# A three-layer transformer stack on one core: head sums as two bulk-format products, waits by eighths, reciprocals and decay tables placed elsewhere

## The chip, the core and the metric

One core of a Trainium2 chip. Five engines work side by side, each through its own list of instructions, and meet only at semaphores: TensorE (PE, matrix products into PSUM), VectorE (DVE), ScalarE (ACT), GpSimd (POOL) and SyncE (SP), which here issues the weight transfers. The metric is the device time of one execution in microseconds; the profile is of one execution of its own, whose time stands beside its span below.

## The reference

A sequence of 512 tokens with 1024 features passes through one block of one kind and two of another. Cut to what matters here:

```python
h = rms_norm(x); proj = h @ w_in                     # block 1
o_attn = dilated_attention(q, k, v)                  # 24 heads of 64; q and k are normed head by head
o_gla  = rms_norm(gated_linear_attention(...)) * silu(r)
x += (gate0 * (o_attn @ w_attn_branch) + gate1 * (o_gla @ w_gla_branch)) @ w_out
x += square(relu(rms_norm(x) @ w_ff_up)) @ w_ff_down
# block 2, layer 0: window attention (8 q heads, 2 kv heads) and neighbourhood attention (8 heads),
#          q and k of both normed head by head;  x += concat(oa, ob) @ w_out_e;  x += mlp(x)
# block 2, layer 1: retention, both directions, 8 heads, decays from per-head rates:
dmask = where(allowed, exp(lg * max(diff, 0)), 0); cross = exp(lg * (pos + 1)); zeta = exp(lg * (127 - pos))
x += (silu(g) * groupnorm(y_f + y_b)) @ w_out_o;  x += mlp(x)
```

Norming q and k head by head means that for each column of 64 values `x * rsqrt(mean(x*x) + eps)` is needed: a sum of squares over each group of 64 features. "Head sum" below is this sum.

## The kernel before

The activations lie transposed in SBUF: `x` is eight tiles of 128 features by 512 tokens. The program runs stage by stage: `l1` (block 1's attention, gated linear attention (GLA), gates and mix), `ff0`, `l2` (window and neighbourhood attention), `ff1`, `l3` (retention), `ff2`.

**Units.** All dense products are cut into units of 128 output columns. A unit has 8 (some 4) slices of 128 inputs, and each slice takes three products in fp32r, the format in which the bulk of the work runs: weight high half by activation high half, high by low, low by high. That makes 24 (or 12) products into one PSUM bank, banks 0 and 1 in turn (`products`, L1529). SP loads a unit's weights, ACT makes their high halves (`split_hi`, L637), DVE their low halves (`split_lo`, L956), both two units ahead. DVE takes a finished unit out of PSUM (`evacuate`, L987, L977, L1008; `post` then finishes it, L1103 for what is added to `x`).

**Order within a step.** `pipeline` makes a list of steps (unit, unit before, parts) for each stage. Each engine walks through it in `static`, and what it does in a step has a fixed order written out in the code. On PE the "parts" (attention, GLA or retention work) and `shared_bank` (a head sum or a transpose of the unit before) are put between the unit's products at positions that `mark` computes; with a shared part the first position (`lead`) is after 10 products. On ACT a step begins with `split_hi` and then finishes the unit before; on DVE it begins with `evacuate`, then `split_lo`, then `post` and the parts.

**Head units.** 37 units are of kind "head": 24 in `l1` (dilated q and k), 5 "a" and 8 "b" in `l2`. DVE evacuates, ACT squares into `tmp` (L647), PE multiplies with `bones`, a matrix of two 64x64 blocks of ones, in fp32 (L1558) into bank 6 (`XB`), ACT takes logarithm and exponential (L649, L651), DVE multiplies (`post`, L1086).

**Dilated attention.** For each item of `l1` the parts are 0 (scores; `softmax` with the sum on DVE, exponentials on ACT, L740), 2 (`normalise`: DVE's reciprocal L1231, which releases POOL's multiplication L552 of the probabilities), 3 (transposes L1650 and their copies) and 1 (product with v, L1679; `head_lo` on DVE, L1238). In `static` of DVE the reciprocal of part 2 stands behind `split_lo`.

**Waits for whole operands.** `operands_ready` in PE's `static` waits before the first product of `w_gla_branch` for all eight output tiles of the GLA (`gl_out`, L1392), and before the three groups of `w_out_o_2` for 8, 12 and 16 tiles of the retention (`ret_out`, L1184). A unit of `w_gla_branch` is multiplied with its gate and added up on DVE, which ends in L1032.

**Layer 3.** `rates(0)` in the second step of `head(0)` has DVE make the exponents of all decay tables (`r_tab`; L1116 to L1131); ACT takes their exponentials in step 4. A retention head runs as six parts (`ret`), one to a step of a later unit; head 7's six go with the first six of the eight units of `w_out_o_2`'s second group.

Of the kernel before, what the change touches and what calls it, by code (L numbers as in the profile page):

```python
# [11 lines left out]
P = 128  # L12
# [51 lines left out]
def plan():  # L64
# [110 lines left out]
    todo = list(zip(head(0), [None, ("rates", 0), None, ("rates", 1), None, None]))  # L175
# [7 lines left out]
    todo += zip([("down", "w_out_o_2", D, P * j, 4, j) for j in range(KD)], ret[7] + [None] * 2)  # L183
# [9 lines left out]
def build(nc, a, out, units, steps):  # L193
    with ExitStack() as ctx:
# [19 lines left out]
        bones = sb("bones", [P, P])  # L214
# [5 lines left out]
        squares = stage[:, 0, :]  # L220
        psum = ctx.enter_context(nc.psum_tensor("psum", [P, 8, 512], F32))
# [16 lines left out]
        head_sq, up_hi, gate_abs = sem("head_sq"), sem("up_hi"), sem("gate_abs")  # L238
        gate_ln, gate_log, gate_exp = sem("gate_ln"), sem("gate_log"), sem("gate_exp")
# [224 lines left out]

        block = ctx.enter_context(nc.Block())
# [40 lines left out]
        def _(pool):  # L506
# [10 lines left out]
            done(pool.memset(bones[:, :], 0.0))  # L517
            for i in range(2):
                done(pool.memset(bones[64 * i:64 * i + 64, 64 * i:64 * i + 64], 1.0))
# [107 lines left out]
        def _(act):  # L627
# [11 lines left out]
            def continue_with(u, more=0):  # L639
# [3 lines left out]
                if u in EVACU and kind != "turn":  # L643
# [59 lines left out]
            def rates(i):  # L703
# [8 lines left out]
                else:  # L712
# [129 lines left out]
            def static(name):  # L842
# [108 lines left out]
        def _(dve):  # L951
# [36 lines left out]

            def post(u, f=0):
# [120 lines left out]
            def rates(i):  # L1110

                if i == 1:
                    return
                dve.wait_ge(rate_ready, 1)
                dve.wait_ge(dist_ready, 3)
                dve.scalar_tensor_tensor(out=r_lg, in0=r_lg, scalar=0.0, in1=r_lt, op0=ALU.min,  # L1116
                                         op1=ALU.subtract).then_inc(dve_step, 1)
                dve.wait_ge(dve_step, chain.up())
                dve.tensor_scalar(r_lt, r_lg, -1.0, None, ALU.mult).then_inc(dve_step, 1)
                dve.wait_ge(dve_step, chain.up())  # L1120

                for h in range(HEADS):
                    dve.tensor_scalar(r_tab[:, h, :], r_dist, r_lt[:, 8 + h:9 + h], None, ALU.mult)
                    dve.tensor_scalar(r_tab[:, HEADS + h, :], r_pos, r_lg[:, h:h + 1], None, ALU.mult)
                    dve.tensor_scalar(r_tab[:, 2 * HEADS + h, :], r_rev, r_lg[:, 8 + h:9 + h], None, ALU.mult)
                dve.tensor_scalar(r_z[:, 0:8], r_lg[:, 0:8], r_dist[:, P - 1:P], None, ALU.mult)
                dve.tensor_scalar(r_z[:, 8:16], r_lt[:, 8:16], r_dist[:, 0:1], None, ALU.mult)
                dve.tensor_scalar(r_z[:, 16:32], r_lg, float(P), None, ALU.mult).then_inc(dve_step, 1)
                dve.wait_ge(dve_step, chain.up())
                for h in range(HEADS):  # L1130
                    ins = dve.scalar_tensor_tensor(out=r_tab[:, h, :], in0=r_dist, scalar=r_lg[:, h:h + 1], in1=r_tab[:, h, :],  # L1131
                                                   op0=ALU.mult, op1=ALU.min)
# [780 lines left out]
```

## Time and profile before

| | us |
|---|---|
| median of 3 runs | 2435.39 (2432.76 to 2435.58) |
| the profiled execution | 2433.26 |
| its span, first to last instruction | 2431.5 |
| mean granted TensorE clock | 0.998 |
| busy: PE, DVE, ACT, POOL | 2388.0, 1261.3, 932.0, 135.4 |

How it is read: the page gives each engine's busy time, the chain of work that ended last, and the costliest groups of instructions by line. The trace behind it can be asked for the instructions of a stretch in order of time (start, duration, engine, line, output <- inputs, and in brackets how long the engine had stood before it and what released it), for what an engine waited for in sum, and for the busy time and granted clock in chosen windows. Matmuls are pipelined: a product's record is longer than the distance to the next one's start, and it is the distance that costs time.

### The profile page before, as it was taken

To read this page: it belongs to the slowest core of one execution; us is meant where nothing else is said; L and a number is where in the kernel's file an instruction comes from. 1 tells how busy PE (TensorE), PEld (TensorE's weight loads), DVE (VectorE), ACT (ScalarE), POOL (GpSimd) and SP (SyncE) were. 2 spreads that over 40 slices of the span, in tenths; PEclk is the share of its full clock that TensorE was granted. 3 is DMA by queue.
4 is the path that set the end of the run, shared out by engine and by line. 5 is a ranking of instruction groups with operands and counts; after the bars stand their busy time and mean duration, and the time that the engine had idled before them with its cause. 6 is when DMAs were issued, how large, how long until landed. Compare 5 with 4: busy or idle time off the path is not lost.

```text
span 2431.5 us, 32682 instructions
## 1 busy us (share of the span) xinstructions
PE 2388.0 (98%) x13012; PEld 1924.1 (79%) x13012; DVE 1261.3 (52%) x1853; ACT 932.0 (38%) x1459; POOL 135.4 (6%) x197
## 2 busy tenths in 40 slices
PE   8999999999999999998999999999999999999999
PEld 5777777787788888875678888887887887888887
DVE  5444444877653433546665344355655556534433
ACT  5343463446342332436654223343332223422321
POOL 3000000000000000042221000000000000100000
PEclk9999999999999999999999999999999999999999
DMA  4222213221323322331023233222222212333322
GB/s 148 71 69 70 70 51 98 77 72 62 104 87 98 107 89 95 104 96 44 23 83 111 89 95 104 88 94 78 70 78 78 87 53 67 110 100 105 95 86 78
DMA packets 60638, 205.79 MB, mean 85 GB/s; under 512 B 7249, under 2 KB 7249, under 8 KB 60386
## 3 DMA queue, kind: packets, MB, share of 16 engines
q1 hardware_dynamic: 59760, 202.93, 26.2%
q8 instruction: 86, 1.41, 0.2%
q10 hardware_dynamic: 754, 1.14, 0.2%
q14 instruction: 38, 0.31, 0.0%
HBM read 201.94 MB, written 2.10 MB: 84 GB/s over the span
## 4 chain that ended last, share of the span: by engine, by line
PE 90%; DVE 5%; ACT 4%; issue 1%; POOL 0%; DMA 0%; SPq 0%; POOLq 0%; DVEq 0%; ACTq 0%
PE psum L1529 79%; PE psum L1558 1%; PE psum L1583 1%; ACT arena L740 1%; PE psum L1554 1%; PE psum L1679 1%; PE psum L1590 1%; PE psum L1673 1%; PE psum L1650 1%; PE psum L1632 1%; DVE arena L1212 0%; DVE cols L1218 0%; ACT whi L637 0%; PE psum L1600 0%; PE psum L1596 0%
## 5 line engine op out<-in xcount | busy, mean ns | idle before, releaser
L1529 PE MATMUL psum<-hhi,whi 128*128 128x512 f32 x1640 | 648.5, 395 | 15.5 <-DVE wlo L956 9.0
L1529 PE MATMUL psum<-hlo,whi 128*128 128x512 f32 x1640 | 655.4, 400 | 0.0
L1529 PE MATMUL psum<-hhi,wlo 128*128 128x512 f32 x1640 | 644.4, 393 | 0.0
L1529 PE MATMUL psum<-uhi,whi 128*128 128x512 f32 x1392 | 548.9, 394 | 5.8 <-DVE arena L1008 2.9
L1529 PE MATMUL psum<-ulo,whi 128*128 128x512 f32 x1392 | 551.7, 396 | 0.0
L1529 PE MATMUL psum<-uhi,wlo 128*128 128x512 f32 x1392 | 547.5, 393 | 0.0
L956 DVE TENSOR_TENSOR wlo<-raw,whi 128x1024 fp32r<-128x1024 f32 (+1 forms) x399 | 465.5, 1167 | 63.3 <-ACT whi L921 31.6
L1529 PEld LDWEIGHTS psum<-hhi,whi 128*128 128x128 f32 x1640 | 308.7, 188 | 84.4 <-issue 14.4
L1529 PEld LDWEIGHTS psum<-hhi,wlo 128*128 128x128 f32 x1640 | 308.8, 188 | 70.1 <-issue 6.8
L1529 PEld LDWEIGHTS psum<-hlo,whi 128*128 128x128 f32 x1640 | 309.1, 188 | 67.9 <-issue 6.7
L921 ACT CAST whi<-raw 128x1024 fp32r<-128x1024 f32 x190 | 199.7, 1051 | 351.9 <-PE psum L1529 351.9
L1529 PEld LDWEIGHTS psum<-uhi,whi 128*128 128x128 f32 x1392 | 262.2, 188 | 66.4 <-issue 8.9
L1529 PEld LDWEIGHTS psum<-uhi,wlo 128*128 128x128 f32 x1392 | 262.2, 188 | 57.6 <-issue 4.9
L1529 PEld LDWEIGHTS psum<-ulo,whi 128*128 128x128 f32 x1392 | 262.2, 188 | 57.2 <-issue 5.1
L1103 DVE TENSOR_TENSOR x<-x,psum 128x512 f32<-128x512 f32 x144 | 99.0, 687 | 352.8 <-PE psum L1529 352.5
L637 ACT CAST whi<-raw 128x1024 fp32r<-128x1024 f32 (+1 forms) x209 | 200.0, 963 | 212.6 <-PE psum L1529 212.5
L977 DVE SCALAR_TENSOR_TENSOR stage<-psum,rstd 128x512 f32<-128x512 f32 x96 | 66.4, 692 | 265.9 <-PE psum L1529 255.5
L665 ACT ACTIVATE tmp<-stage 128x512 f32<-128x512 f32 x96 | 60.7, 632 | 310.5 <-DVE stage L977 310.5
L987 DVE TENSOR_TENSOR stage<-psum,rstd 128x512 f32<-128x512 f32 (+1 forms) x118 | 85.5, 724 | 130.5 <-PE psum L1529 126.9
L552 POOL TENSOR_TENSOR arena<-arena,cols 128x512 f32<-128x512 f32 (+4 forms) x48 | 58.6, 1220 | 384.1 <-DVE cols L1231 383.9
L1107 DVE TENSOR_TENSOR hlo<-tmp,hhi 128x512 fp32r<-128x512 f32 x96 | 66.5, 692 | 20.3 <-ACT hhi L667 20.3
L740 ACT ACTIVATE arena<-arena,cols 128x256 f32<-128x256 f32 (+4 forms) x96 | 52.1, 544 | 58.2 <-DVE cols L1216 58.2
(220 smaller groups left out, 1692.3 us busy)
## 6 DMA issues: line engine op xcount, KB each, us to landing
raw<-in_packed_dram SPq DMA_DIRECT2D x359, 512.0 KB, 3.6
raw<-in_packed_dram SPq DMA_DIRECT2D x40, 256.0 KB, 2.5
x<-in_xt_dram SPq DMA_DIRECT2D x8, 256.0 KB, 8.1
out_dram<-x SPq DMA_DIRECT2D x8, 256.0 KB, 2.0
arena<-in_near_bias_dram ACTq DMA_DIRECT2D x1, 1024.0 KB, 5.7
vec<-in_vec_dram ACTq DMA_DIRECT2D x1, 44.0 KB, 4.1
arena<-in_gla_gate_up_dram ACTq DMA_DIRECT2D x1, 32.0 KB
arena<-in_gla_gate_bias_dram ACTq DMA_DIRECT2D x1, 2.0 KB
```

The lines of the kernel that those rows point to most:

```text
L552: pool.tensor_tensor(p, p, part, ALU.mult).then_inc(att_norm, 1)
L637: nc.scalar.copy(whi[:, u % 4, 0:kt, :], raw[:, u % 4, 0:kt, :]).then_inc(hi_done, 1)
L665: nc.scalar.activation(t, s, ACT.Square).then_inc(act_step, 1)
L740: ins = nc.scalar.activation(p[:, i, :], p[:, i, :], ACT.Exp, bias=c[:, i:i + 1], accum_out=c[:, 2 + i:3 + i])
L921: nc.scalar.copy(whi[:, u % 4, :, :], raw[:, u % 4, :, :]).then_inc(hi_done, 1)
L956: dve.tensor_tensor(wlo[:, u % 4, 0:kt, :], raw[:, u % 4, 0:kt, :], whi[:, u % 4, 0:kt, :].bitcast(F32), ALU.subtract).then_inc(lo_done, 1)
L977: dve.scalar_tensor_tensor(out=s, in0=g, scalar=0.0, in1=rstd, op0=ALU.max, op1=ALU.mult).then_inc(evacuated, 1)
L987: dve.tensor_tensor(s, g, r, ALU.mult).then_inc(evacuated, 1)
L1103: dve.tensor_tensor(x[:, j, :], x[:, j, :], g, ALU.add).then_inc(posted, 1)
L1107: dve.tensor_tensor(lo[:, j, :], tmp[:, u % 2, :], hi[:, j, :].bitcast(F32), ALU.subtract)\
L1529: mm = pe.matmul(g, w[:, u % 4, k, :], v[:, k, :], start=n == 0, stop=n == 3 * kt - 1)
L1554: mm = pe.transpose(XB[:, P * t:P * t + P], src, ident[:, :])
```

## The change

It does six things.

1. **Head sum in two products of fp32r.** ACT squares the evacuated unit into a high half (the last tile of the operand buffer that is free in that stage), DVE multiplies the unit with itself in fp32 into `tmp` and subtracts the high half, which gives the low half. PE multiplies `bones` (now fp32r, copied once by DVE) with the high, then the low half, into the same bank.
2. **Order on ACT and DVE.** ACT's square comes ahead of `split_hi`; DVE's multiplication and subtraction come ahead of `split_lo`.
3. **Lead.** With a head unit before, the shared part stands after 13 products instead of 10.
4. **Reciprocals.** In `l1` the reciprocal of part 2 comes ahead of these squares instead of behind `split_lo`.
5. **Waits by eighths.** The full waits of `operands_ready` go; each slice of the first unit waits for its own tile.
6. **Retention.** `rates` is spread over four steps (1 to 4 of `head(0)`), ACT's exponentials remain in the last of them; head 7's parts go with units 0, 2, 4 (two of them), 5 and 6.

```diff
-    todo = list(zip(head(0), [None, ("rates", 0), None, ("rates", 1), None, None]))
+    todo = list(zip(head(0), [None] + [("rates", i) for i in range(4)] + [None]))
...
-    todo += zip([("down", "w_out_o_2", D, P * j, 4, j) for j in range(KD)], ret[7] + [None] * 2)
+    r = ret[7]
+    todo += zip([("down", "w_out_o_2", D, P * j, 4, j) for j in range(KD)],
+                [r[0], None, r[1], None, [r[2], r[3]], r[4], r[5], None])
...
+        def head_squares(u):
+            hi, lo = first_operand if units[u][5][0] in ("a", "b") else second_operand
+            return hi[:, KD - 1, :], lo[:, KD - 1, :]
...
-                    nc.scalar.activation(t, s, ACT.Square).then_inc(head_sq, 1)
...
+            def square_head(u):                                  # ACT
+                act.wait_ge(evacuated, EVACU[u] + 1)
+                nc.scalar.activation(head_squares(u)[0], stage[:, u % 2, :], ACT.Square).then_inc(head_sq, 1)
...
                 for u, prev, parts in steps[name]:               # ACT static
+                    if prev is not None and units[prev][0] == "head":
+                        square_head(prev)
                     if u is not None:
                         split_hi(u + 2)
...
+            def square_head(u):                                  # DVE
+                s, t = stage[:, u % 2, :], tmp[:, u % 2, :]
+                hi, lo = head_squares(u)
+                dve.wait_ge(evacuated, EVACU[u] + 1)
+                dve.tensor_tensor(t, s, s, ALU.mult).then_inc(dve_step, 1)
+                dve.wait_ge(dve_step, chain.up())
+                dve.wait_ge(head_sq, HEADU[u] + 1)
+                dve.tensor_tensor(lo, t, hi.bitcast(F32), ALU.subtract).then_inc(head_low, 1)
...
                     if prev is not None:                         # DVE static
                         evacuate(prev)
+                    for part in parts:
+                        if part[:2] == ("att", "dil") and part[3] == 2:
+                            normalise(run_at["dil"] + part[2])
+                    if prev is not None and units[prev][0] == "head":
+                        square_head(prev)
...
                         split_lo(u + 2, kt=units[u + 2][4])
-                    for part in parts:
-                        if part[:2] == ("att", "dil") and part[3] == 2:
-                            normalise(run_at["dil"] + part[2])
...
+                    if u in outputs_before and part == 0:        # PE products
+                        pe.wait_ge(ret_out, outputs_before[u] + k + 1)
+                    if u == gla_branch0 and part == 0:
+                        pe.wait_ge(gl_out, k + 1)
...
-                    pe.matmul(XB, bones[:, :], tmp[:, u % 2, :], start=True, stop=True).then_inc(head_sum, 1)
+                    pe.matmul(XB, bones[:, :], hi, start=True, stop=False)
+                    pe.wait_ge(head_low, HEADU[u] + 1)
+                    pe.matmul(XB, bones[:, :], lo, start=False, stop=True).then_inc(head_sum, 1)
...
-                    lead = 10 if shared and not soon else 0
+                    lead = 0 if soon or not shared else 13 if units[prev][0] == "head" else 10
```

In `rates`, step 0 now makes the rates and the small columns (5 operations), step 1 the 16 operations of `cross` and `zeta`, step 2 eight of the mask's exponents, step 3 the eight L1131.

## Rows read from the trace of the kernel before

**Rows 1.** The page: busy time by engine, and the chain by engine.
```profile
PE 2388.0 (98%) x13012; PEld 1924.1 (79%) x13012; DVE 1261.3 (52%) x1853; ACT 932.0 (38%) x1459; POOL 135.4 (6%) x197
...
PE 90%; DVE 5%; ACT 4%; issue 1%; POOL 0%; DMA 0%; SPq 0%; POOLq 0%; DVEq 0%; ACTq 0%
```
**Rows 2.** PE's waits: line, releaser: us in total, times, longest.
```profile
PE psum L1558 <- ACT tmp L647: 8.0, 6, 3.2
...
PE psum L1759 <- DVE arena L1341: 2.4, 1, 2.4
...
PE psum L1650 <- POOL arena L552: 1.5, 3, 0.6
```
**Rows 3.** Timeline of PE, layer 1: start, us, engine, line, out<-in.
```profile
78.78 0.39 PE L1529 MATMUL psum<-hhi,whi 128*128 128x512 f32 x1
...
79.69 1.02 PE L1558 MATMUL psum<-tmp,bones 128*128 128x512 f32 x2
...
80.78 0.40 PE L1529 MATMUL psum<-hhi,wlo 128*128 128x512 f32 x1
```
**Rows 4.** Groups by line and form: count, busy, mean ns, idle before.
```profile
L1107 DVE TENSOR_TENSOR hlo<-tmp,hhi 128x512 fp32r<-128x512 f32 x96 | 66.5, 692 | 20.3 <-ACT hhi L667 20.3
...
L647 ACT ACTIVATE tmp<-stage 128x512 f32<-128x512 f32 x37 | 23.3, 630 | 24.5 <-DVE stage L987 24.2
```
**Rows 5.** Timeline of PE, DVE and POOL in a step with a reciprocal.
```profile
101.07 0.39 PE L1529 MATMUL psum<-hhi,whi 128*128 128x512 f32 x1
...
101.64 0.68 DVE L987 TENSOR_TENSOR stage<-psum,rstd 128x512 f32<-128x512 f32 x1
...
103.61 1.47 POOL L552 TENSOR_TENSOR arena<-arena,cols 128x768 f32<-128x768 f32 x1 [14.99 <-DVE cols L1231]
```
**Rows 6.** Timeline of DVE and POOL in layer 2 and behind it.
```profile
1089.67 0.71 DVE L1192 TENSOR_SCALAR arena<-arena 128x384 f32<-128x384 f32 x2
...
1112.21 1.45 DVE L1192 TENSOR_SCALAR arena<-arena 128x384 f32<-128x384 f32 x2
...
1112.38 1.08 POOL L552 TENSOR_TENSOR arena<-arena,cols 128x512 f32<-128x512 f32 x1 [4.06 <-DVE cols L1231]
...
1278.52 1.44 POOL L613 TENSOR_TENSOR stage<-stage,tmp 128x512 f32<-128x512 f32 x1 [1.41 <-ACT tmp L886]
...
1279.51 1.00 DVE L1442 SCALAR_TENSOR_TENSOR ulo<-x,vec,uhi 128x512 fp32r<-128x512 f32 x1
```
**Rows 7.** Layer 3: timeline of DVE and PE, then a window's busy times, PEclk, DMA.
```profile
1642.28 0.29 DVE L1123 TENSOR_SCALAR arena<-arena 128x128 f32<-128x128 f32 x1
...
1649.56 1.22 DVE L956 TENSOR_TENSOR wlo<-raw,whi 128x1024 fp32r<-128x1024 f32 x1
...
1648.23 0.39 PE L1529 MATMUL psum<-uhi,wlo 128*128 128x512 f32 x1
1651.53 0.77 PE L1529 MATMUL psum<-uhi,whi 128*128 128x512 f32 x1 [2.91 <-DVE arena L1008]
...
1651.00:1658.00 7.00, 6.47 (x18) 5.20 (x19) 3.05 (x5) 2.69 (x4) 0.00 (x0) 0.52 0.48 150
```
**Rows 8.** Timeline of PE at the first group of w_out_o_2.
```profile
1843.45 0.39 PE L1529 MATMUL psum<-uhi,wlo 128*128 128x512 f32 x1
1846.93 0.47 PE L1529 MATMUL psum<-hhi,whi 128*128 128x512 f32 x1 [3.09 <-DVE hlo L1184]
```
**Rows 9.** Timeline of PE and DVE at the last retention head.
```profile
2028.21 2.61 PE L1583 MATMUL psum<-arena 128*128 128x256 f32 x11 [2.59 <-issue]
...
2029.22 0.68 DVE L1103 TENSOR_TENSOR x<-x,psum 128x512 f32<-128x512 f32 x1
```
**Rows 10.** Timeline of PE, third unit of w_gla_branch.
```profile
621.84 0.47 PE L1529 MATMUL psum<-uhi,whi 128*128 128x512 f32 x1 [1.63 <-DVE hlo L1032]
```
**Rows 11.** Windows behind two other stalls: busy by engine, PEclk, DMA.
```profile
582.00:586.00 4.00, 3.09 (x10) 2.64 (x11) 3.61 (x6) 3.65 (x7) 0.00 (x0) 0.57 0.22 75
2020.00:2030.00 10.00, 7.20 (x37) 5.70 (x36) 8.47 (x16) 5.52 (x10) 0.00 (x0) 1.00 0.09 30
```

More of the change, by code:

```diff
@@ L213, in build @@
         ones = sb("ones", [P, P])
-        bones = sb("bones", [P, P])
+        bones = sb("bones", [P, P], F32R)
         vec = sb("vec", [P, VALL])
@@ L220, in build @@
         squares = stage[:, 0, :]
+        bones_in = arena[:, 16800:16800 + P]
         psum = ctx.enter_context(nc.psum_tensor("psum", [P, 8, 512], F32))
@@ L516, in _ @@
             done(pool.memset(const[:, 1:2], GN_EPS))
-            done(pool.memset(bones[:, :], 0.0))
+            done(pool.memset(bones_in, 0.0))
             for i in range(2):
-                done(pool.memset(bones[64 * i:64 * i + 64, 64 * i:64 * i + 64], 1.0))
+                done(pool.memset(bones_in[64 * i:64 * i + 64, 64 * i:64 * i + 64], 1.0))
             done(pool.memset(ident[:, :], 0.0))
@@ L642, in continue_with @@
                 s, t = stage[:, u % 2, :], tmp[:, u % 2, :]
-                if u in EVACU and kind != "turn":
+                if u in EVACU and kind not in ("turn", "head"):
                     act.wait_ge(evacuated, EVACU[u] + 1 + more)
                 if kind == "head":
-                    nc.scalar.activation(t, s, ACT.Square).then_inc(head_sq, 1)
                     act.wait_ge(head_sum, HEADU[u] + 1)
@@ L711, in rates @@
                     nc.scalar.activation(r_lt, r_lt, ACT.Ln, bias=1.0).then_inc(rate_ready, 1)
-                else:
+                if i == 3:
                     act.wait_ge(ret_exp, 1)
@@ L1110, in rates @@
             def rates(i):
-                if i == 1:
[L1113 to L1132, printed above, removed]
-                ins.then_inc(ret_exp, 1)
+                if i == 0:
+                    dve.wait_ge(rate_ready, 1)
+                    dve.wait_ge(dist_ready, 3)
+                    dve.scalar_tensor_tensor(out=r_lg, in0=r_lg, scalar=0.0, in1=r_lt, op0=ALU.min,
+                                             op1=ALU.subtract).then_inc(dve_step, 1)
+                    dve.wait_ge(dve_step, chain.up())
+                    dve.tensor_scalar(r_lt, r_lg, -1.0, None, ALU.mult).then_inc(dve_step, 1)
+                    dve.wait_ge(dve_step, chain.up())
+                    dve.tensor_scalar(r_z[:, 0:8], r_lg[:, 0:8], r_dist[:, P - 1:P], None, ALU.mult)
+                    dve.tensor_scalar(r_z[:, 8:16], r_lt[:, 8:16], r_dist[:, 0:1], None, ALU.mult)
+                    dve.tensor_scalar(r_z[:, 16:32], r_lg, float(P), None, ALU.mult)
@@ new lines, in rates @@
+                if i == 1:
+                    for h in range(HEADS):
+                        dve.tensor_scalar(r_tab[:, HEADS + h, :], r_pos, r_lg[:, h:h + 1], None, ALU.mult)
+                        dve.tensor_scalar(r_tab[:, 2 * HEADS + h, :], r_rev, r_lg[:, 8 + h:9 + h], None, ALU.mult)
+                if i == 2:
+                    for h in range(HEADS):
+                        ins = dve.tensor_scalar(r_tab[:, h, :], r_dist, r_lt[:, 8 + h:9 + h], None, ALU.mult)
+                    ins.then_inc(dve_step, 1)
+                    dve.wait_ge(dve_step, chain.up())
@@ L1135, in ret @@
+                if i == 3:
+                    for h in range(HEADS):
+                        ins = dve.scalar_tensor_tensor(out=r_tab[:, h, :], in0=r_dist, scalar=r_lg[:, h:h + 1],
+                                                       in1=r_tab[:, h, :], op0=ALU.mult, op1=ALU.min)
+                    ins.then_inc(ret_exp, 1)
             def ret(h, part):
@@ L1489, in _ @@
             dve.tensor_scalar(nbias[:, :], vec[:, b0:b0 + 16], -1.0, None, ALU.mult).then_inc(vec_ready, 1)
+            dve.tensor_copy(bones[:, :], bones_in).then_inc(bones_ready, 1)
             q_norms = vec[:, VROWS:VROWS + 6].rearrange("p (a b) -> p a b", b=2)[:, :, 0]
@@ L1510, in _ @@
                             UNIT_OF["down", "w_out_e_2", 512, 0]: "near"}
+            outputs_before = {UNIT_OF["down", "w_out_o_2", 0, 0]: 0, UNIT_OF["down", "w_out_o_2", D, 0]: 8,
+                              UNIT_OF["down", "w_out_o_2", D + 4 * P, 0]: 12}
             norm_before = {first(n[0]): i for i, n in enumerate(NORMS)}
@@ L1796, in _ @@
                      "shared_bank": shared_bank}
-            def operands_ready(u):
-                names = units[u][:4]
-                if names == ("branch", "w_gla_branch", 0, 0):
-                    pe.wait_ge(gl_out, 8)
-                if names == ("down", "w_out_o_2", 0, 0):
-                    pe.wait_ge(ret_out, 8)
-                if names == ("down", "w_out_o_2", D, 0):
-                    pe.wait_ge(ret_out, 12)
-                if names == ("down", "w_out_o_2", D + 4 * P, 0):
-                    pe.wait_ge(ret_out, 16)
             def mark(i, n, total, lead):
```

5 lines of the change are left out of this document (4 added, 1 removed).

## The prediction

> **What bounds the kernel now.** I read the page's busy shares and its chain of waits first: TensorE (PE) is busy 98% of the span and makes 90% of the chain, VectorE (DVE) 52%, ScalarE (ACT) 38%, GpSimd (POOL) 6% [rows 1]. So the time is PE's work plus the places where PE stands. Second, PE's waits, longest first: outside the start, which the change doesn't touch, PE stands in pieces of at most 3.2 us at a few dozen places [rows 2, 7 to 10]. Third, PE's timeline around one head sum, for what PE itself pays: products start 0.227 us apart (four from 78.78 to 79.69), and from the start of the head sum at 79.69 to the second product behind it 1.09 us go by; less one product that is 0.86 us for a head sum, two fp32 records [rows 3]. There are 37 of them. An edit brings something only if it makes PE's own work shorter or ends a stall that nothing else holds. The sum below is made against the profiled execution, 2433.26 us with a span of 2431.5. The median of the runs, 2435.39, lies 2.1 above it, which I add at the end.
>
> **Head sums, PE's side.** The fp32 pass (0.86) goes, two fp32r products come. The fp32r products here start 0.227 apart, so two cost 0.45; saved 0.41 each, 37 times: **15.2** gain. The trace has no fp32r product with this stationary matrix; the bounds are a price as now (0 saved) and 0.45, and I take 0.45, since form and sizes are those of the 128x512 products beside it.
>
> **Head sums, the other engines.** ACT's square (630 ns) is done ahead of the weight split instead of behind it. DVE gets a multiplication and a subtraction of 128x512 in front of its weight split; the like of it, two SBUF sources, takes 692 ns [rows 4]. PE now reaches the head sum 13 products into the unit and its second half at 14, that is 3.17 us after the unit begins. Evacuation of the unit before ends 1.25 us in at most where the attention isn't late [rows 5] (normally sooner), so the low half is there at 1.25 + 1.4 = 2.65: hidden by 0.5 us. The weight split that is queued behind them comes 1.4 later, but is for a unit two further on. Were all this cover gone, 37 x 1.4 = 52 us would appear; DVE's 52% speaks against it. The first heads of each stage, where the norm is late, gain a little: **0.5** (0 to 1).
>
> **Reciprocals ahead of the squares.** In nine of the 24 dilated heads (three in each of three groups) the item's reciprocal now stands directly in front of the multiplication and the subtraction. It releases POOL's normalising multiplication (L552), which in [rows 5] started in DVE's idle time and took 1.47 us. What the two engines do to each other is in [rows 6]: the pair of operations L1192 takes 0.71 us at 1089.67, with no L552 beside it, and 1.45 at 1112.21, where POOL's L552 (from 1112.38, 1.08 us) begins between the two; the second is through 0.2 behind POOL's end. And an L1442 under POOL's L613 takes 1.00, where the like takes 0.69 [rows 4], and ends 0.55 behind POOL's end, as if it had stood until then. I take this: the operation that comes second stands until the first is done. Then, for the middle head of three, counted from the unit's begin at 101.07: scores run 0.27 later than now (three products later, 0.68, less 0.41), so evacuation ends at 1.25 + 0.27 = 1.52, the reciprocal is through at 1.7, the multiplication (issued before POOL) at 2.4, POOL at 3.9, the subtraction at 4.6. PE wants it at 3.17: it stands 1.45. With the last head's longer L552 (1.68) and 0.15 later evacuation it is 1.8; with the first's shorter one (0.83) and its evacuation that is not held up by the attention, 0.35. Three of each, less what stands there now (0.2, 0, 0): **-0.5 - 4.35 - 5.4 = -10.2**. Bounds: 0 (no conflict) and -12.
>
> The Trainium skill ("SBUF — State Buffer", section "Who interferes with whom") says that a DVE instruction with two SBUF inputs and a GpSimd instruction that reads SBUF contend for a shared port pair, and that the one issued first keeps the other out. It speaks against this part of the change, and the rows agree with it: 10.2 us lost. If the added operations had one SBUF input each, by that rule nothing would be lost here.
>
> **Layer 2's eight 'b' heads.** PE stands 8.0 us in six pieces at the head sum, waiting for ACT's square, up to 3.2 [rows 2]. The square in front of the 1.05 us split takes about 0.8 to 1.0 off the larger ones; but DVE's two added operations delay the weight split, softmax and the masks that POOL makes there, which share the port. I take +4.3 and give back 3.3: **+1.0**, bounds -4 and +3.
>
> **GLA gates, first block.** Three stalls of PE behind POOL's L552, 1.5 us together [rows 2]: with the reciprocal ahead of the weight split the first goes, the others stay a little because POOL now meets the split's port use: **+1.0** (0 to 1.8).
>
> **Eighths.** For w_gla_branch PE may start as soon as the first eighth is out. But two units on it waits 1.63 us for L1032, a chain of ACT and DVE that does not hang on PE [rows 10]; starting earlier makes that wait longer by as much: **0** (0 to 0.8). For w_out_o_2, PE stands from 1843.45 + 0.23 to 1846.93, 3.25 us, for the last of eight outputs [rows 8]; this one is needed only with the last of the unit's eighths, 21 products = 4.8 us later. No other wait is listed at this place: **+3.25** (0 to 3.25).
>
> **Decay tables.** In the second step of layer 3 DVE works from 1642.28 to 1649.56 on tables (24 operations like the one of 1642.28, then 11 more), and the weight split and L1008 queue behind it; PE stands from 1648.23 + 0.23 to 1651.53, 3.07 us. After that the granted clock is 0.52, the lower of its two levels (1.2 GHz), in 1651 to 1658 [rows 7]: of the 6.47 us that PE is busy there, 0.48 each is lost, some 3.0 more (an estimate from this row). Spread over four steps, no step gets more than 16 of the 35 operations, 3.4 us of the 7.3, so L1008 is some 4 to 5 us sooner, ahead of 1648.2. The tables are first wanted by the first retention head, four units on; by the operations of each step they are ready shortly before PE comes there (0.4 us, an estimate from the spacing of the steps). Gain **6.0** (if the clock falls anyway or the tables are late: 3).
>
> **Last retention head.** PE's stall of 2.59 (L1583) is put down to issue; what it follows is the retention work on DVE [rows 9]. With the parts moved a step on, unit 2 begins not before L1103, which now ends at 2029.90, has freed the bank. PE had six products of the unit done and stood from about 2025.5; it would come to unit 2 at 2026.8 and stand to about 2030, 3.2 instead of 2.75: **-0.4** (-1.5 to 1.5). The copy of the bones at the start lies in DVE's idle time before the first norm: 0.
>
> **Sum**: 15.2 + 0.5 - 10.2 + 1.0 + 1.0 + 0 + 3.25 + 6.0 - 0.4 = 16.3. 2433.26 - 16.3 = 2417.0, and 2.1 to the median: **2419**.
>
> **The rivals.**
> *No conflict at the port.* The subtraction runs beside POOL, the nine stalls don't come: 10.2 better, **2408.8**. For it: no row shows a subtraction of this very form beside L552, and the order of arrival may differ. Against: both conflicts in [rows 6].
> *DVE binds in the attention parts.* The 1.4 us more per head on DVE delay softmax, scores and masks in layers 1 and 2 as well, each time by what the lower bounds above hold (-4 instead of +1 in layer 2, and 1 us more): **2425**.
> *The stalls of layer 3 move instead of going.* As with w_gla_branch, the next wait takes up the 9.25 us: **2428**.
> *No cheaper pass.* If two fp32r passes with the bones cost what one of fp32 costs, 15.2 goes and the rest (1.1) remains: **2434**, no change that can be told.
> *Slower: the clock falls behind the new stalls.* After the 3.07 stall in layer 3 and after the 2.4 us wait at L1341 the clock fell to its lower level for some us (0.52 and 0.57 [rows 2, 7, 11]), 3.0 lost at the first. If each of the nine new stalls of layer 1 did this, 26 us would be added: **2445**; it decides from the sixth such fall on (16.3 / 3.0). Against it: the stall of 2.59 in 2020 to 2030 left the clock at 1.00 [rows 11], and so would most of 0.35 to 1.8.
>
> **How the numbers follow.** Chances: the forecast (2413 to 2423) 0.50; no conflict 0.20; DVE binds 0.13; layer 3 gives back 0.08; no cheaper pass 0.04; slower 0.05. The range 2407 to 2428 takes in the first three cases, and half of the fourth, with the bounds of the layer 2 and layer 3 terms on either side. About 0.2% (4.9 us) is what a measurement of this kernel can tell from no change. Faster by more: the first four cases, less a little, 0.88; within: "no cheaper pass" and the edges of its neighbours, 0.07; slower: 0.05.
>
> **What would show it.** In the profile after: head sums with two products 0.23 apart instead of 0.86 in all (right), or still 0.4 apart (wrong). In layer 1, PE waits at the head sum's second product for DVE's subtraction, nine times, 1 to 2 us each, with an L552 in front of it on POOL: if these are missing, the conflict was misjudged and the time is near 2409. In layer 3 the waits on L1008 and L1184 gone, the granted clock at 1.00 in 1651 to 1658 and no new wait of their size within the next two units; if one is there, the gain moved. In layer 2 the head sum's waits for ACT under 4 us in sum. In the first block's branch the wait on L1032 longer by what the one before it lost. The prediction is wrong as a whole if the weight splits (L956) appear among PE's waits for more than a few us: then DVE's added work isn't covered.

## The result

| | before | after |
|---|---|---|
| median of 4 runs each, us | 2434.89 | 2419.93 (2419.79 to 2420.46) |
| ratio to before (95% interval) | | 0.994 (0.9923 to 0.9958) |
| profiled execution, us | 2433.26 | 2420.46 |
| its span, us | 2431.5 | 2418.5 |

The change makes the kernel 15.0 us faster by the medians and 12.8 by the two profiled executions; 2419 was forecast. One of the four executions of experiment 8 below took 4598.90 us at a granted clock of 0.911 and is left out of its median. The page's busy line and its chain, after:

```profile
PE 2374.2 (98%) x13012; PEld 1924.0 (80%) x13012; DVE 1322.5 (55%) x1928; ACT 932.9 (39%) x1459; POOL 152.6 (6%) x197
...
PE 86%; DVE 6%; ACT 4%; POOL 2%; issue 2%; DMA 0%; POOLq 0%; SPq 0%; DVEq 0%; ACTq 0%
```

Beside [rows 1]: PE works 13.8 us less, DVE 61 us more, and POOL 17 us more although it has the same 197 instructions. PE's share of the chain falls from 90% to 86%, POOL's rises from 0 to 2%. Most of this 2% is masks in layer 2 (L601, 32 us of the chain) and not the normalising that the forecast was about (L561, 4.9 us in layer 1, 4.4 before), so it is no sign of the nine stalls. Those show in PE's waits, after (in sum, times, longest):

```profile
...
PE psum L1602 <- DVE ulo L1010: 9.4, 10, 1.6
PE psum L1568 <- DVE x L1126: 4.4, 2, 3.1
PE psum L1568 <- DVE hlo L1055: 2.5, 1, 2.5
PE psum L1803 <- DVE arena L1368: 2.5, 1, 2.5
...
PE psum L1600 <- ACT hhi L679: 2.1, 2, 1.7
PE psum L1694 <- POOL arena L561: 1.9, 3, 1.3
```

Line numbers have moved: L1568 is the products' line (L1529 before), L1600 and L1602 the two products of the head sum, L1007 and L1010 DVE's multiplication and subtraction, L561 POOL's normalising (L552), L1126 the addition to `x` (L1103), L1055 the end of a branch unit (L1032). The head sum's wait for ACT fell from 8.0 [rows 2] to 2.1. The waits on L1008 and L1184 [rows 7, 8] are gone. New, and the largest but for the start, is the wait that was forecast: L1602 for the subtraction, nine of its ten times at the heads behind a reciprocal (9.2 of the 9.4 us). The weight splits (L970), whose appearance was to show the prediction wrong as a whole, hold PE up for 0.8 us beyond the 8.9 at the start (9.0 before): DVE's added work is covered there. Where the decay tables made PE stand in [rows 7], it now works through, at the full clock (after):

```profile
1643.00:1647.00 4.00, 4.00 (x22) 3.28 (x21) 3.08 (x5) 0.95 (x1) 0.00 (x0) 1.00 0.30 73
```

A head sum where nothing is late (timeline of PE, after): the two products are 0.22 and 0.23 apart from their neighbours, 0.45 for the sum, where [rows 3] had 0.86.

```profile
29.45 0.39 PE L1568 MATMUL psum<-hhi,whi 128*128 128x512 f32 x1
29.68 0.39 PE L1600 MATMUL psum<-uhi,bones 128*128 128x512 f32 x1
29.90 0.39 PE L1602 MATMUL psum<-ulo,bones 128*128 128x512 f32 x1
30.13 0.39 PE L1568 MATMUL psum<-hlo,whi 128*128 128x512 f32 x1
```

And a step with a reciprocal (all engines, after), to be read against [rows 5]:

```profile
97.90 0.69 DVE L1001 TENSOR_TENSOR stage<-psum,rstd 128x512 f32<-128x512 f32 x1
...
98.50 0.16 DVE L1258 RECIPROCAL cols<-cols 128x2 f32<-128x2 f32 x1
...
98.62 0.69 DVE L1007 TENSOR_TENSOR tmp<-stage 128x512 f32<-128x512 f32 x1
...
98.73 1.90 POOL L561 TENSOR_TENSOR arena<-arena,cols 128x768 f32<-128x768 f32 x1 [14.96 <-DVE cols L1258]
...
99.35 1.83 DVE L1010 TENSOR_TENSOR ulo<-tmp,uhi 128x512 fp32r<-128x512 f32 x1
...
99.62 0.39 PE L1600 MATMUL psum<-uhi,bones 128*128 128x512 f32 x1
...
101.24 0.50 PE L1602 MATMUL psum<-ulo,bones 128*128 128x512 f32 x1 [1.23 <-DVE ulo L1010]
```

The reciprocal releases POOL at 98.66, while the multiplication already runs. POOL's L561 takes 1.90 instead of 1.47, and the subtraction, issued at 99.35, takes 1.83 instead of 0.69 and ends 0.55 behind POOL's end at 100.63. PE stands 1.23 between the two products of one head sum. By the starts of the products this stall costs 1.50: 1.39 between the two, where 1.62 lie instead of 0.227, and 0.11 behind them, where 0.34 lie. A wait as the profile lists it begins at the end of a record of 0.39, and so leaves 0.27 of the stall's price out.

### The profile page after: what moved, and what is told of

Its sections match the earlier page's. It is cut to its first block, busy times and chain, and to the rows that moved or that the text cites. A ratio compares the mean times of both kernels' runs of the same rounds, so it can differ in the third digit from the quotient of the medians.

```text
span 2418.5 us, 32796 instructions
## 1 busy us (share of the span) xinstructions
PE 2374.2 (98%) x13012; PEld 1924.0 (80%) x13012; DVE 1322.5 (55%) x1928; ACT 932.9 (39%) x1459; POOL 152.6 (6%) x197
## 4 chain that ended last, share of the span: by engine, by line
PE 86%; DVE 6%; ACT 4%; POOL 2%; issue 2%; DMA 0%; POOLq 0%; SPq 0%; DVEq 0%; ACTq 0%
PE psum L1568 77%; POOL arena L601 1%; ACT arena L752 1%; PE psum L1627 1%; PE psum L1593 1%; DVE ulo L1010 1%; PE psum L1723 1%; PE psum L1694 1%; PE psum L1634 1%; DVE stage L1001 1%; PE psum L1676 1%; PE psum L1644 0%; PE psum L1640 0%; PE psum L1602 0%; DVE cols L1243 0%
## 5 line engine op out<-in xcount | busy, mean ns | idle before, releaser
L1568 PE MATMUL psum<-hhi,whi 128*128 128x512 f32 x1640 | 647.8, 395 | 15.4 <-DVE wlo L970 9.7
L1568 PE MATMUL psum<-hlo,whi 128*128 128x512 f32 x1640 | 645.0, 393 | 0.0
L1568 PE MATMUL psum<-hhi,wlo 128*128 128x512 f32 x1640 | 644.5, 393 | 0.0
L1568 PE MATMUL psum<-uhi,whi 128*128 128x512 f32 x1392 | 548.3, 394 | 3.1 <-DVE hlo L1055 2.5
L1568 PE MATMUL psum<-uhi,wlo 128*128 128x512 f32 x1392 | 545.7, 392 | 0.0
L1568 PE MATMUL psum<-ulo,whi 128*128 128x512 f32 x1392 | 545.0, 392 | 0.0
L970 DVE TENSOR_TENSOR wlo<-raw,whi 128x1024 fp32r<-128x1024 f32 (+1 forms) x399 | 465.8, 1168 | 60.7 <-ACT whi L935 31.5
L1568 PEld LDWEIGHTS psum<-hhi,whi 128*128 128x128 f32 x1640 | 308.6, 188 | 83.5 <-issue 10.9
L1568 PEld LDWEIGHTS psum<-hhi,wlo 128*128 128x128 f32 x1640 | 308.8, 188 | 64.7 <-issue 1.0
L1568 PEld LDWEIGHTS psum<-hlo,whi 128*128 128x128 f32 x1640 | 309.1, 189 | 63.6 <-issue 1.0
L1568 PEld LDWEIGHTS psum<-uhi,whi 128*128 128x128 f32 x1392 | 261.6, 188 | 62.7 <-issue 8.8
L1568 PEld LDWEIGHTS psum<-uhi,wlo 128*128 128x128 f32 x1392 | 261.6, 188 | 55.3 <-issue 1.8
L1568 PEld LDWEIGHTS psum<-ulo,whi 128*128 128x128 f32 x1392 | 261.8, 188 | 54.1 <-issue 2.0
L1126 DVE TENSOR_TENSOR x<-x,psum 128x512 f32<-128x512 f32 x144 | 98.9, 687 | 348.1 <-PE psum L1568 347.8
L561 POOL TENSOR_TENSOR arena<-arena,cols 128x512 f32<-128x512 f32 (+4 forms) x48 | 67.2, 1400 | 361.3 <-DVE cols L1258 361.1
```

Source lines behind the costliest of these rows:

```text
L561: pool.tensor_tensor(p, p, part, ALU.mult).then_inc(att_norm, 1)
L970: dve.tensor_tensor(wlo[:, u % 4, 0:kt, :], raw[:, u % 4, 0:kt, :], whi[:, u % 4, 0:kt, :].bitcast(F32), ALU.subtract).then_inc(lo_done, 1)
L1126: dve.tensor_tensor(x[:, j, :], x[:, j, :], g, ALU.add).then_inc(posted, 1)
L1568: mm = pe.matmul(g, w[:, u % 4, k, :], v[:, k, :], start=n == 0, stop=n == 3 * kt - 1)
```

## Where the time went, product by product

The dense products are the same in number and order in both kernels, so the distance between the same two products before and after gives what each part did (two profiled executions; positive is gained):

| part | forecast | measured |
|---|---|---|
| 37 head sums on PE | 15.2 | 16.6 (0.45 each) |
| first head of each stage | 0.5 | 0.3 |
| nine heads behind a reciprocal | -10.2 | -11.5 |
| layer 2, the eight 'b' heads beyond that | +1.0 | -1.3 |
| GLA gates | +1.0 | +1.35 |
| w_gla_branch by eighths | 0 | +0.86 - 0.90 = 0 |
| decay tables | 6.0 | 6.0 (3.07 of stall + 2.94 of clock) |
| first group of w_out_o_2 by eighths | 3.25 | 3.4 |
| last retention head | -0.4 | -2.1 |
| start and rest | 0 | 0.3 |
| sum | 16.3 | 13.1 |

All but two terms are within 1.4 us of the forecast. The two that are not, layer 2 and the last retention head, are where the granted clock fell after the change and hadn't before (experiments 3 and 7). The profiled execution of before lay 1.6 us below its median, that of after 0.5 above: the medians lie 15.0 apart and the profiles 12.8, so 2419.9 and 2419 agree better than the sums behind them (16.3 and 13.1).

## The experiments

Each kernel is the changed one with one edit, unless said otherwise. Medians are of runs beside the kernel before on the same chip. Theory: the nine stalls are a conflict of DVE's subtraction with POOL's normalising; the other losses are the granted clock. Rivals: DVE's queue alone; stalls alone.

**1. The square in PSUM.**

```diff
-                s, t = stage[:, u % 2, :], tmp[:, u % 2, :]
+                s, t = stage[:, u % 2, :], psum[:, u % 2, :]
...
-                    if u - 2 in EVACU:
+                    if u - 2 in HEADU:
+                        pe.wait_ge(head_low, HEADU[u - 2] + 1)
+                    elif u - 2 in EVACU:
```

> The changed kernel, but DVE puts the product s*s into the PSUM bank of the unit just taken out instead of into SBUF, so that the subtraction has one SBUF source. Theory (the subtraction stands because POOL's L561 holds what both need for a second SBUF source): the subtraction takes 0.69 us beside L561 instead of 1.4 to 2.0, the nine waits at the head sum's second product in layer 1 (9.2 us, 11.2 by starts) shrink to 0.2 each, time about 2410. Rival (DVE's order is what makes them late, whatever the sources): the waits stay, 2420. In layer 2, where the masks run on POOL, the theory also lets some of the 2 us in waits there go.

2410.57 us (ratio 0.990, 0.9885 to 0.9915): 9.4 less than after. The same step:

```profile
97.90 0.15 DVE L1258 RECIPROCAL cols<-cols 128x2 f32<-128x2 f32 x1
...
98.01 0.70 DVE L1007 TENSOR_TENSOR psum<-stage 128x512 f32<-128x512 f32 x1
...
98.13 1.90 POOL L561 TENSOR_TENSOR arena<-arena,cols 128x768 f32<-128x768 f32 x1 [14.52 <-DVE cols L1258]
...
98.75 0.69 DVE L1010 TENSOR_TENSOR ulo<-psum,uhi 128x512 fp32r<-128x512 f32 x1
...
99.01 0.39 PE L1602 MATMUL psum<-uhi,bones 128*128 128x512 f32 x1
...
99.49 0.50 PE L1604 MATMUL psum<-ulo,bones 128*128 128x512 f32 x1
...
99.62 1.49 DVE L970 TENSOR_TENSOR wlo<-raw,whi 128x1024 fp32r<-128x1024 f32 x1 [0.18 <-ACT whi L646]
```

Order and number of instructions are the same; what has changed is where the product lies, which the multiplication writes and the subtraction reads (and PE waits for the subtraction before it fills that bank again; no wait of the profile is put down to this). The subtraction takes 0.69 in the middle of POOL's 1.90. Over all 24 heads its mean goes from 1.07 to 0.69 us, and PE's wait at the second product in 77 to 400 us from 9.2 to this:

```profile
PE psum L1604 <- DVE ulo L1010: 0.7, 3, 0.2
```

The rival is out: the conflict is between two SBUF sources on DVE and POOL. The weight split (two SBUF sources) still stands for 0.27 us at the end of POOL's instruction, 1.49 against 1.22, and L561 keeps its 1.90, since the multiplication still reads SBUF twice (experiment 11 takes it away). In layer 2, where the theory had hoped for some of 2 us, the profile gained 0.9, part of it because the clock was low for a shorter time there; the profile of experiment 12, with the clock as long down as after, gained 0.4.

**2. The reciprocal behind the weight split again.**

```diff
-                    for part in parts:
-                        if part[:2] == ("att", "dil") and part[3] == 2:
-                            normalise(run_at["dil"] + part[2])
                     if prev is not None and units[prev][0] == "head":
                         square_head(prev)
...
                         split_lo(u + 2, kt=units[u + 2][4])
+                    for part in parts:
+                        if part[:2] == ("att", "dil") and part[3] == 2:
+                            normalise(run_at["dil"] + part[2])
```

> The changed kernel with the reciprocals of the dilated attention behind the weight split again, as before the change. Theory: the nine waits at the head sum (11.2 by starts) go, but POOL now begins at about 4.6 us into the unit and PE stands at the transposes L1694 some 0.9 to 1.1 us in six steps: about 2415. Rival (POOL has nothing to do with it; the two added DVE operations alone are late): the nine waits stay and the transposes wait on top, 2425 or more.

2420.9 us: no gain. PE's waits in the first 290 us of layer 1 show that the place was right and the sum wrong:

```profile
PE psum L1694 <- POOL arena L561: 6.1, 6, 1.1
PE psum L1602 <- DVE ulo L1010: 1.0, 5, 0.2
```

The 9.2 at the head sum went down to 1.0, and 6.1 came at the transposes, each 0.9 to 1.1 as expected; the net is 2.1 by waits, and 0.8 by starts (there are more stalls, and each costs more than its wait), not the 5 that I had made of it by setting the losses by starts (11.2) against gains by waits. The GLA gates gave another 1.3 back. With the square in SBUF, POOL is either in the subtraction's way or late for the transposes; the reciprocal's place only chooses which.

**3. The last retention head as before.**

```diff
-                [r[0], None, r[1], None, [r[2], r[3]], r[4], r[5], None])
+                r + [None] * 2)
```

> The changed kernel with the last retention head's six parts on units 0 to 5 again. Theory (the lower clock level after the 3.1 us stall costs the 1.4 there, the stalls themselves 0.5): the granted clock stays at 1.00 in the 5 us behind the stall and the time is 1.9 lower, 2418. Rival (the clock falls behind any stall of this kind): 2419.5, with the clock at 0.66 behind the stall again.

2419.86 us in the median (2417.68 to 2420.96), which doesn't tell it from after; the profiled execution, 2417.68, is 2.8 below that of after, 2.1 of it in this place. What the clock did there (first line after, behind the stall that ends at 2014.87; second line this kernel, behind the one at 2012; busy by engine, PEclk, DMA):

```profile
2015.00:2020.00 5.00, 5.00 (x16) 4.04 (x17) 1.94 (x5) 0.00 (x0) 0.00 (x0) 0.66 0.36 105
```
```profile
2012.00:2017.00 5.00, 4.64 (x29) 4.36 (x30) 4.79 (x11) 0.48 (x1) 0.00 (x0) 1.00 0.18 52
```

So the 2.1 lost in the last retention head are some 0.5 of stall (3.07 instead of 2.59), as forecast, and some 1.6 of clock: seven products 0.43 apart behind it make 1.4. The profile of experiment 4 separates the two: PE stands 3.08 there, the clock stays at 1.00 in 2021 to 2026, and the place loses 0.4 against before. That this holds in every run isn't shown by a median that didn't move.

**4. Lead 10.** The head sum stands after 10 products of the next unit again: `lead = 0 if soon or not shared else 10`.

> The changed kernel with the head sum after 10 products of the next unit instead of 13. If the low half is ready 0.5 us early at 13, as I worked out (2.65 against 3.17 us), it is ready 0.15 late or just in time at 10: PE waits up to 0.2 us at each of the 15 undisturbed heads of layer 1 and more in layer 2; time 2420 to 2425. Rival (the attention behind the head sum gains 0.68 from the earlier scores): 2417 or less.

2424.83 us, 4.9 more than after, as expected (2420 to 2425). The three later products are worth that: with 10, PE waits longer at L1600 for ACT's square in layer 2 (2.9 us by starts there), and a little at each head of layer 1 (2 us there in all).

```profile
PE psum L1600 <- ACT hhi L679: 4.7, 4, 2.5
```

**5. Decay tables in one step.** The list of steps as before, all four parts of `rates` in part 0.

> The changed kernel with all of DVE's decay tables in one step again. Theory: 3.1 us of stall at L1031 or so come back and the granted clock falls to its lower level behind it, 6.0 together: 2426. Rival (the clock fell in the profile of before by chance and not behind this stall): only 3.1 come back, 2423, with the clock at 1.00 behind it.

2426.46 us, 6.5 more than after. Timeline of PE and the window behind:

```profile
1645.72 0.47 PE L1568 MATMUL psum<-uhi,whi 128*128 128x512 f32 x1 [2.91 <-DVE arena L1031]
```
```profile
1645.00:1650.00 5.00, 4.28 (x15) 3.46 (x15) 2.31 (x3) 2.89 (x4) 0.00 (x0) 0.68 0.62 175
```

The stall is the one of [rows 7] to the hundredth, and the clock falls behind it again, for a shorter time (3.1 and 1.7 by starts, 4.8 in the profile; 2.9 of clock before). Most of the other 1.2 by which the two profiles differ is a longer fall at the last retention head. The rival is out: the three profiles with this stall (before, 5, 9) have a fall behind it, the eleven without have none, and both parts of the 6.0 were real.

**6. Full waits.** In `products` the first product waits for all `kt` tiles of `gl_out` and `ret_out`.

> The changed kernel with the waits for whole operands again at w_gla_branch and w_out_o_2. Theory: w_out_o_2 costs its 3.25 again and w_gla_branch nothing, because the wait for L1055 two units on (2.5 us now) shrinks by what is lost ahead of it: 2423.2. Rival (w_gla_branch's eighths bring what they remove, 0.8): 2424.

2425.18 us, 5.2 more, and 2 above what was expected. At w_gla_branch the small stall comes back and the next one shrinks (PE, this kernel; after has none and 2.49):

```profile
607.84 0.47 PE L1568 MATMUL psum<-uhi,whi 128*128 128x512 f32 x1 [0.61 <-DVE ulo L1419]
...
620.59 0.47 PE L1568 MATMUL psum<-uhi,whi 128*128 128x512 f32 x1 [1.59 <-DVE hlo L1055]
```

0.61 + 1.59 against 2.49: the eighths of the GLA bring nothing, as forecast. At w_out_o_2 the 3.09 came back, and this time the clock fell behind it, 0.66, which it hadn't done in the profile of before; that cost 1.6 more by starts. The stall and the clock:

```profile
1834.47 0.47 PE L1568 MATMUL psum<-hhi,whi 128*128 128x512 f32 x1 [3.09 <-DVE hlo L1211]
```
```profile
1834.00:1839.00 5.00, 4.53 (x14) 3.64 (x14) 4.11 (x7) 1.89 (x3) 0.00 (x0) 0.66 0.24 87
```

**7. Fewer masks.** Four of the six calls of `within` on POOL taken out.

> The changed kernel with 32 of the 48 mask operations of POOL (L601) in layer 2 left out: the bias of the neighbourhood attention stays partly unmasked. Theory (layer 2 loses its gain because DVE's added operations and POOL's masks hold each other up, so that the first 'b' head's square and the first item's normalising are late, 1.7 and 1.35 us, and the granted clock falls to 0.5 to 0.7 behind these two): both waits shrink below 1 us in sum, the clock stays at 1.00 from 1090 to 1108, and layer 2 is 4 to 5 us shorter, time about 2415. Rival (the chain from exponentials to square to head sum is that long by itself): the waits stay and the time is within 1 us of 2420.

2418.64 us, 1.3 less. Between theory and rival: the wait of 1.35 at the transposes went, the one at the first 'b' head's square stayed at 1.54 (1.72), so the masks aren't what holds that one. The clock (first line after, second this kernel):

```profile
1097.00:1104.00 7.00, 5.65 (x19) 2.86 (x20) 4.66 (x9) 3.03 (x9) 4.26 (x5) 0.53 0.29 75
```
```profile
1097.00:1104.00 7.00, 6.77 (x41) 4.54 (x41) 5.13 (x11) 4.73 (x12) 1.75 (x2) 1.00 0.23 75
```

At 0.53 after, 1.00 here, and 1.00 in 1096 to 1104 before: in layer 2 PE's waits fell by 2.2 us with the change (10.7 to 8.5), more than I had expected, and the clock took part of that back in the profiled execution (5.65 busy at 0.53: 2.7 of slower work). The price is less than the 2.7: experiments 8 and 12, one kernel without and with this fall, lie 1.3 apart in layer 2 by starts, since PE, when it is slower, has less to wait for behind it (0.3 instead of 1.1 for POOL's L561). That the masks draw the fall isn't shown: with all of them the clock stayed at 1.00 in the profile of experiment 8 too.

**8. Squares in PSUM, and another order in the last group of layer 3** (on top of experiment 1).

```diff
-                [r[0], None, r[1], None, [r[2], r[3]], r[4], r[5], None])
+                [None, r[0], r[1], None, [r[2], r[3]], r[4], r[5], None])
...
+                    down = prev is not None and units[prev][0] == "down"
+                    if down:
+                        post(prev)
                     if u is not None:
                         split_lo(u + 2, kt=units[u + 2][4])
...
-                        post(prev)
+                        if not down:
+                            post(prev)
```

> The kernel with squares in PSUM, and in the last group of layer 3 the first part of the last retention head on unit 1 instead of unit 0, the second on unit 2, and DVE adding a finished unit to x ahead of the weight split. Theory: PE's 3.1 us stall behind the addition of unit 0 shrinks to 1.6 (0.85 from the part, 0.6 from the order), and the clock doesn't fall behind it, 3 us together: 2407.5. Rival (the next wait of the retention chain takes it up): 2410, with the waits in 2025 to 2040 longer by as much.

2408.42 us in the median of three executions (ratio 0.9889, 0.9871 to 0.9907), and 2407.58 when it was timed once more (below). The stall and the clock behind it:

```profile
2000.24 0.47 PE L1572 MATMUL psum<-hhi,whi 128*128 128x512 f32 x1 [1.58 <-DVE stage L1001]
```
```profile
2000.00:2005.00 5.00, 4.40 (x25) 3.59 (x25) 2.87 (x6) 4.05 (x8) 0.00 (x0) 1.00 0.17 52
```

1.58 as worked out, no fall, 2.9 gained by starts against experiment 1, and no later wait of the retention grew by as much: the rival is out. It is some 12 us faster than the changed kernel.

**9. The head sums alone** (the kernel before, with parts 1 to 3 of the change).

> The kernel before with only the head sums changed (two fp32r products, ACT's square and DVE's two operations in their new places, lead 13); reciprocals, waits, decay tables and last head as before. By the forecast's terms alone (0.41 each on 37 heads, 0.5, and 1 in layer 2) it would be 17 lower, 2418. Theory from the runs so far (with the reciprocal behind the weight split POOL is late for the transposes, some 9 us in layer 1; layer 2 gives back 1 to 3): 4 to 6 lower, 2429 to 2431. Rival: 2418.

2427.38 us, 6.8 below before (2434.2), a little more than the 4 to 6 expected, and far from the rival's 2418. Of the 16.6 that PE saves on its own work, less than half arrives: PE's waits in the same stretch of layer 1 as in experiment 2 are again 6.1 and 1.0. Without a price for POOL the forecast's sum for this part would not hold.

**10. The high half alone.** No multiplication, no subtraction, no second product; the low halves are left out.

> The changed kernel without DVE's multiplication and subtraction and without the second product: the head sum takes the rounded squares alone, the low halves are left out. If DVE's two operations cost nothing but the nine stalls, 8.4 (37 products of 0.227) and 11 go and the time is 2400.5. Rival (DVE's operations bind in layer 2 as well, by the order of the queue and the port): layer 2 is 3 or more shorter on top, 2397 or less. Second rival (the nine stalls come from POOL and ACT, not from the subtraction): 2411.

2396.99 us, 22.9 below after. The theory's 2400.5 is missed by 3.5, and the time is the rival's, but not for the rival's reason alone: 8.4 are the 37 products, layer 1 gave 12.5 beyond its 24 products (11 expected) and layer 2 2.0 beyond its 13, not 3 or more. So DVE's two operations cost the changed kernel some 14.5 us, the nine stalls (11.5) and some 3 us more. Experiment 1 got 9.1 of this back in layer 1 without leaving anything out.

**11 and 12. ACT squares twice, DVE only subtracts (on top of experiment 8); and experiment 8 once more.**

```diff
-                nc.scalar.activation(head_squares(u)[0], stage[:, u % 2, :], ACT.Square).then_inc(head_sq, 1)
+                nc.scalar.activation(head_squares(u)[0], stage[:, u % 2, :], ACT.Square)
+                nc.scalar.activation(psum[:, u % 2, :], stage[:, u % 2, :], ACT.Square).then_inc(head_sq, 1)
...
-                dve.tensor_tensor(t, s, s, ALU.mult).then_inc(dve_step, 1)
```

> The kernel with squares in PSUM and the new order in layer 3, and ACT squares twice (rounded into the high half, and in fp32 into the unit's PSUM bank), so that DVE only subtracts. Theory (DVE's multiplication, two SBUF sources, still holds POOL's L561 up by 0.4 to 0.5 us and binds a little in layer 2): L561 takes 1.47 instead of 1.9, layer 2 gains 1, but the square comes 0.63 later for PE where ACT is late, five times: within 1.5 us of the 2408.7 of the kernel without this. Rival (ACT's order binds in the attention): 2412 or more.

> The kernel with squares in PSUM and the new order in layer 3 once more, beside the one above: 2408.7, and below the 2410.6 of squares in PSUM alone.

2414.43 and 2407.58 us: 6.8 worse, the rival. PE's waits with two squares on ACT:

```profile
PE psum L1604 <- ACT psum L680: 5.8, 10, 2.5
```

DVE's multiplication runs beside ACT's square; on one engine the two are a chain, and it ends too late. The edit also makes PE's first product wait for both squares, although it needs only the first, since only the second signals; how much of the 6.8 is due to that wasn't measured. The theory's other half holds: without DVE's multiplication POOL's L561 takes in the step of [rows 5] what it took before the change, 1.47 instead of 1.90,

```profile
98.99 1.47 POOL L561 TENSOR_TENSOR arena<-arena,cols 128x768 f32<-128x768 f32 x1 [15.04 <-DVE cols L1256]
```

but PE's waits for L561 had been only 0.9 us in experiment 12 and are 0.6 here.

## Why the prediction was right, and where not

*PE's own work.* Right, with 16.6 instead of 15.2: 0.45 a head sum. The "no cheaper pass" rival is out by the timeline.

*The reciprocals ahead of the squares.* Right in cause, place and size: nine stalls of 0.2, 1.2 to 1.3 and 1.5 to 1.6 us by waits, 9.2 in all, and 11.5 by starts. The step that carried it was the reading of two conflicts in [rows 6], and experiment 1 shows it by changing only where one source lies. The Trainium skill ("SBUF — State Buffer", "Who interferes with whom") says the same, and says that the first to issue keeps the other out: in the step shown, POOL waits for the multiplication (1.90 instead of 1.47), then the subtraction for POOL (1.83 instead of 0.69). Its remark that a DVE instruction with at most one SBUF input, outside the two-port modes, doesn't contend is what experiment 1 measures, 0.69 us beside L561. One source alone is no safe rule, though: L1192, the first of the two conflicts in [rows 6], is a TENSOR_SCALAR with a single tensor source, and the second of its pair still took 1.20 beside L552, where 0.34 was its time without. So only the other row, L1442, was a case of two sources, and the prediction read both as one kind. The "no conflict" rival is out.

*Layer 2.* Right that DVE's extra work gives back part of the shorter wait for ACT; wrong in the term's sign (+1.0 forecast, -1.3 measured, inside the bounds of -4 and +3). The step that failed is that I priced stalls alone. By waits alone the term is about +2; the clock behind them, which I had only as the "slower" rival for layer 1, took some 1.3 here (experiments 8 and 12). Without the fall the term would be about 0 (an estimate from these two numbers), and not 1 or 2. Part of the rest may be that a stall costs more than its wait, and the profile after has two stalls more in layer 2 than that of before (15 and 13); the remainder stays open. The "DVE binds" rival has a little in it: the 3 us that experiment 10 found beyond the stalls. What is known of which stalls draw a fall is in the last section.

*Gates, branch, tables, outputs.* Right, to 0.4 us. The w_gla_branch wait moved two units on, to the tenth. The stalls of layer 3 went and didn't move, so the rival in which that layer gives back its 9.25 is out.

*Last retention head.* The stall was right (0.5 longer, 0.4 forecast), the clock behind it, some 1.6, was not priced. I had seen that the stall of 2.59 left the clock alone [rows 11] and didn't ask whether one of 3.07 would. This is the term at fault.

*The slower rival* took the clock to fall behind the nine stalls of layer 1. None of these was followed by a fall in any profile; it fell behind other, longer ones.

*What the medians add.* That the forecast of 2419 met 2419.9 so closely is in part luck. I had added the 2.1 between before's profile and its median, and the profile of after lies above its own median; profile against profile, 2417.0 was forecast and 2420.46 came.

## What to carry to other kernels

When an engine's added instruction is priced at its own duration, ask what the instruction in front of it releases: here a reciprocal released POOL into the very time in which DVE needed its second SBUF source, and two thirds of the gain on PE went into it. Moving one source to PSUM, into a bank that is free anyway, took the conflict with the subtraction away at no wait that the profile shows; moving the reciprocal only moved it. And price a stall of PE of 1.5 to 3 us with the clock behind it, as a cost that comes in some executions and not in others, less what the next wait takes back.

## What the runs showed of the hardware

How often the granted clock fell to its lower level within some 9 us behind a wait of PE (windows of 3 us, 0.9 or less), over the profiles of this case that have the wait:

| wait, us | where | fell in |
|---|---|---|
| 0.2 to 1.6 | nine heads of layer 1 (after, 3 to 7) | 0 of 6 |
| 1.6 | last group of layer 3 (8, 11, 12), third branch unit (before, 6, 9) | 0 of 6 |
| 1.5 to 2.5 | first 'b' head of layer 2, changed kernels | 11 of 13 |
| 3.2 | the same place before, one fp32 head sum | 0 of 1 |
| 2.4 to 2.5 | GLA, ending at 564 to 584 | 9 of 14 |
| 2.5 | third branch unit, ending at 603 to 623 | 5 of 11 |
| 2.6 | last group of layer 3 (before, 3, 9) | 0 of 3 |
| 2.9 | decay tables (before, 5, 9) | 3 of 3 |
| 3.1 | first group of w_out_o_2 (before, 6, 9) | 2 of 3 |
| 3.1 | last group of layer 3 (after, 1, 2, 4 to 7, 10) | 7 of 8 |

What a fall cost depends on what stands behind it. By starts it was 1.6 at the branch, 1.4 to 2.9 in layer 3 and, in layer 2, 1.3 between experiments 8 and 12. At the GLA it was 0 to 0.3: there it held the products up by 1.3 to 1.6 at first, but each of the five profiles without a fall then has one more wait (the line is of experiment 2), and none of the nine with a fall has it.

```profile
PE psum L1811 <- DVE arena L1391: 1.1, 1, 1.1
```

The wait's length alone doesn't decide: 2.6 in one place never drew it, 2.4 in another did in two of three. Nor does the place: the same wait draws it in one execution and not in the next, and the 2.5 at the branch drew it in all four profiles in which the GLA's, 40 us sooner, had not, but in one of seven in which it had. This is one reason why runs of one kernel here lie up to 6 us apart (experiment 5: 2421.8 to 2428.2), and why a term of 2 us is better read from the products of two profiles than from medians. What decides stays open; so does whether the two-product head sums are why layer 2 draws it now, since only one profile of before was there to compare.
